# Unused matmuls ahead of the transposes of eight norms and of sixteen attention heads in a four-layer fp32 kernel

## The reference, cut to what matters

```python
xf = x.astype(jnp.float32)
y = xf * lax.rsqrt(jnp.mean(xf * xf, axis=-1, keepdims=True) + RMS_EPS)
return (y * g.astype(jnp.float32)).astype(x.dtype)
```

```python
p = jnp.where(mask, jnp.exp(s - m), 0.0)
return p / jnp.maximum(jnp.sum(p, axis=-1, keepdims=True), 1e-30)
...
o = g[..., 0:1] * o_c + g[..., 1:2] * o_s + g[..., 2:3] * o_w
```

## Time and profile before

| | |
|---|---|
| time, median of 3 runs | 2771.21 us (2769.89 to 2772.66) |
| the profiled execution's own time | 2782.96 us |
| its span, first to last instruction | 2781.2 us |
| PE busy | 2602.2 us (94%), 15074 records |
| PE weight loads busy | 2178.7 us (78%) |
| DVE, ACT, POOL busy | 1316.1, 398.8, 207.3 us |
| chain of work that ended last | PE 86%, DMA 7%, DVE 4%, ACT 2% |
| granted TensorE clock, mean | 0.939 |
| attention of section four, first scores to last combine | 2350.5 to 2493.3 us |

### The profile page before, as it was taken

How to read it: one execution, slowest core, us unless ns; L and a number is a source line. 1 busy time by engine, 2 the same in 40 slices (tenths; PEclk the granted TensorE clock), 3 DMA queues, 4 the chain that set the end, 5 groups by cost and what they waited for, 6 DMA issues and landing times.

```text
span 2781.2 us, 36057 instructions
## 1 busy us (share of the span) xinstructions
PE 2602.2 (94%) x15074; PEld 2178.7 (78%) x15074; DVE 1316.1 (47%) x2542; ACT 398.8 (14%) x1150; POOL 207.3 (7%) x208
## 2 busy tenths in 40 slices
PE   6998999999999899999999999983899999999998
PEld 5557999999998755899999998872466587875665
DVE  4734928878743473493887874316100001431001
ACT  2121111111100212111111111012000001320000
POOL 0000012222210000001222121000000000000000
PEclk9999999999999999999999999996899997559999
DMA  5222679999999332367999999840244422002432
GB/s 202 98 84 106 242 279 398 389 381 407 416 421 382 133 116 74 114 242 291 408 391 376 401 419 421 360 149 37 91 151 151 170 102 92 1 1 106 151 151 91
DMA packets 84755, 625.33 MB, mean 225 GB/s; under 512 B 10443, under 2 KB 12978, under 8 KB 14206
## 3 DMA queue, kind: packets, MB, share of 16 engines
q1 hardware_dynamic: 55580, 420.85, 39.3%
q0 software_dynamic: 28032, 201.54, 17.9%
q10 hardware_dynamic: 994, 0.82, 0.1%
HBM read 621.91 MB, written 1.06 MB: 224 GB/s over the span
## 4 chain that ended last, share of the span: by engine, by line
PE 86%; DMA 7%; DVE 4%; ACT 2%; issue 1%; SPq 0%; DVEq 0%; ACTq 0%; PEldq 0%
PE bank L716 19%; PE bank L741 16%; PE bank L466 9%; PE bank L480 8%; PE bank L488 8%; PE bank L454 8%; DMA weight_ring<-in_experts 5%; PE bank L730 5%; PE bank L418 3%; PE bank L838 2%; PE bank L904 2%; PE bank L906 1%; PE bank L536 1%; DMA arena<-in_expert_rows,choice_by_pair 1%; ACT arena L956 1%
## 5 line engine op out<-in xcount | busy, mean ns | idle before, releaser
L741 PE MATMUL bank<-arena,weight_ring 128*128 128x160 f32 x4096 | 576.2, 301 | 14.4 <-DMA weight_ring<-in_experts 14.3
L741 PEld LDWEIGHTS bank<-arena,weight_ring 128*128 128x128 f32 x4096 | 558.8, 190 | 25.3 <-DMA weight_ring<-in_experts 23.6
L716 PE MATMUL bank<-hidden_T,weight_ring 128*128 128x160 f32 x4096 | 570.6, 301 | 2.6 <-ACT arena L1065 2.3
L716 PEld LDWEIGHTS bank<-hidden_T,weight_ring 128*128 128x128 f32 x4096 | 561.3, 191 | 3.9 <-issue 3.8
L1615 DVE CUSTOM_DVE_ANT_0 arena<-arena 128x1024 f32<-128x1024 f32 x192 | 234.5, 1221 | 209.0 <-DMA arena<-in_expert_rows,choice_by_pair 208.8
L454 PE MATMUL bank<-weight_ring,hidden_T 128*128 128x512 f32 (+1 forms) x544 | 236.4, 592 | 36.4 <-DVE hidden_T L1734 34.3
L466 PE MATMUL bank<-hidden_T,weight_ring 128*128 128x256 f32 (+1 forms) x1088 | 249.6, 391 | 10.2 <-DMA weight_ring<-in_dense_h 6.1
L944 POOL DMA_INDIRECT arena<-in_expert_rows,choice_by_pair x192 | 200.2, 1043 | 789.0 <-DVE arena L1628 713.2
L466 PEld LDWEIGHTS bank<-hidden_T,weight_ring 128*128 128x128 f32 (+1 forms) x1088 | 208.5, 193 | 46.4 <-issue 7.0
L1628 DVE SCALAR_TENSOR_TENSOR arena<-arena,pair_weights 128x1024 f32<-128x1024 f32 x188 | 240.6, 1280 | 0.2
L480 PEld LDWEIGHTS bank<-hidden_T,weight_ring 128*128 128x128 f32 x1024 | 194.6, 190 | 52.9 <-issue 29.7
(11 more groups left out here) (313 smaller groups left out, 1832.4 us busy)
## 6 DMA issues: line engine op xcount, KB each, us to landing
weight_ring<-in_experts SPq DMA_DIRECT2D x256, 1024.0 KB, 9.2
weight_ring<-in_mlp SPq DMA_DIRECT2D x64, 1024.0 KB, 4.8
weight_ring<-in_dense_h SPq DMA_DIRECT2D x22, 2048.0 KB, 7.6
weight_ring<-in_dense_nsa SPq DMA_DIRECT2D x9, 2048.0 KB, 7.8
weight_ring<-in_dense_rg SPq DMA_DIRECT2D x7, 2048.0 KB, 7.6
arena<-in_expert_rows,choice_by_pair POOLq DMA_INDIRECT x192, 11.2
arena<-distance_bias_scratch SPq DMA_DIRECT2D x2, 768.0 KB, 5.6
residual<-in_x SPq DMA_DIRECT2D x1, 1024.0 KB
```

What stands on the lines that cost most here:

```text
L716: last = mm(bank[s % 2][:, 0:DT_TOK], w[:, k * P:(k + 1) * P], HT[:, k, 0:DT_TOK], start=k == 0, stop=k == KD - 1)
L741: last = mm(bank[4 + k // 2][:, (k % 2) * DT_TOK:(k % 2 + 1) * DT_TOK], w[:, k * P:(k + 1) * P], HACT[:, s, :], start=s == 0 and k % 2 == ...
```

## The change

Both additions are on PE alone and are read by nothing. In each of the eight norms, sixteen 128-column matmuls of the identity by itself go into bank 1 ahead of the wait for `norm_scaled`; the transposes overwrite that bank. In each of the sixteen heads, three matmuls of the identity by 256 columns of zeros go into bank 4, which the head's own transposes overwrite. To make this possible the two waits of `nsa_turn` change places: the one for `nsa_PT` comes first, then the three matmuls, then the one for `nsa_probs`. Line numbers of the kernel after are higher by 2 from L421 on, and by 4 behind `nsa_turn`, ACT and DVE included.

```diff
             def norm(count):
+                for _ in range(16):
+                    mm(bank[1][:, 0:P], ident[:], ident[:], start=True, stop=True)
                 for tt in range(TT):
 
                     pe.wait_ge(S["norm_scaled"], count * TT + tt + 1)
@@ -881,9 +883,11 @@
             def nsa_turn(h):
 
-                pe.wait_ge(S["nsa_probs"], h + 1)
                 if h:
                     pe.wait_ge(S["nsa_PT"], h)
+                for _ in range(3):
+                    mm(bank[4][:, 0:T], ident[:], zrow[:, 0:T], start=True, stop=True)
+                pe.wait_ge(S["nsa_probs"], h + 1)
```

## The result

| | before | with the change |
|---|---|---|
| time, median | 2771.93 us (2769.89 to 2781.58, 4 runs) | 2730.53 us (2728.52 to 2731.61, 4 runs) |
| ratio to before | | 0.9838, 95% interval 0.982 to 0.9857 |
| span of the profiled execution | 2781.2 us | 2729.8 us |
| mean granted clock | 0.939 | 0.973 |

The forecast was 2732 us, in a range from 2712 to 2757. The ratio is a gain of 45 us with an interval of 40 to 50; the medians differ by 41.

The account below looks back on a forecast made before the run. The prediction took TensorE at half its clock to bound the attention. Gains of 26 (attention), 9.5 and 3 (norms) and 1 (behind the attention) sum to 39.5 us: 2771.2 - 39.5 = 2732 us, range 2712 to 2757.

Parts of the forecast that it names:

- The bound: Attention of sixteen heads: TensorE at half its clock bounds the 143 us stage, busy for 138.6 of them.
- What raises the clock: TensorE: unbroken work on all rows raises it, zeros and transposes included; expected within the first one or two heads.
- The rule against it: Trainium skill: transposes don't engage the full clock, leaving a head's unbroken stretch 2.56 us, not 4.27; rival's chance 0.06.
- What lets it fall: TensorE: idle time or thin work, as in the compression, where 4.00 us at 1.00 came before 9.80 at 0.50.
- The price of a head: Attention, with the unused matmuls: a head costs 11.29 us at 1.2 GHz, 6.12 us at 2.4 GHz.
- The share at the low clock: Attention: 0.3 of the time at 1.2 GHz, bounds 0.05 and 0.6; stage gain 26 us.
- the formula: Attention time: sixteen heads at a rate weighting 11.29 and 6.12 us by clock share, plus 3.1 us; forecast 116.6.
- The norms behind a projection: Four norms after output projections: identities hidden in 4.5 us of idle time, clock holds; gain 9.5 us.
- The norms behind a barrier: Four norms behind a barrier: transposes 0.8, 0.8 and 2.0 us later in three, faster dense work; together +3 us.
- Behind the attention: Output projection after the attention, cold for 3.5 us: half of up to 1.8 + 0.7 us gained, +1.
- The sum: Whole kernel: 26 + 9.5 + 3 + 1 = 39.5 us gained, giving a median of 2732 us.

Follow-up runs that it names:

- first trace of before: The profile of the unchanged kernel that the prediction read: profiled execution 2782.96 us, span 2781.2 us.
- split runs: The change with each head's unused matmuls in two places: two and two of 256 columns, 0.9841 to before; three and three of 128 columns, 0.9828.
- heads only: The kernel before plus only the three unused matmuls per head and the exchanged waits, no identities in the norms: 0.9875 to before.
- second trace of before: The kernel before, unchanged, profiled once more: 2774.26 us, span 2772.5 us.

## Why the prediction was right

- **The bound.** TensorE at half its clock in the attention, nothing else near: right. With the clock up TensorE was still the bound, busy for 110.6 of 112.3 us, and neither ACT's copies nor the waits took over.
- **What raises the clock.** Work on all rows, zeros and transposes included: shown, by 64 rows that did not do it and by twelve transposes that did. The rule against it fell. How long the work must be unbroken was not tested apart.
- **What lets it fall.** The prediction read this off the compression's products, and that row bears less than was put on it. Its 4.0 us at 1.00 hold mostly the 48-column records of L454 ahead of the products. And the same 256 records took 13.57 us in the first trace of before, 10.54 in the second, and 10.30 in the kernel after, where the clock stood at 1.00 from 2319.3 to 2329.5 us (timeline of before, then of the kernel after):

```profile
2333.36 13.57 PE L853 MATMUL bank<-arena,weight_ring 64*64 64x45 f32 x256
```

```profile
2319.26 10.30 PE L855 MATMUL bank<-arena,weight_ring 64*64 64x45 f32 x256
```

So thin work does not always let the clock fall: 10 us of it passed at 1.00. That the thin stretch of a head does is shown by the split runs, not by that row. What makes it fall in one head and not in the next stays open, and so does which part of the stretch counts: its values use all rows, with 65 columns each.
- **The price of a head.** 6.12 us at the full clock was forecast, and 6.07 measured. That switches between row groups cost the same 0.2 us at either clock carried this; with them halved it would have been 5.6. The chain after shows it again: eight L908 records take 1.04 us, of which 0.85 are streaming, and at half the clock before they took 1.90, of which 1.71.
- **The share at the low clock.** I chose 0.3, and it was 0.28 in the trace. This was a choice between 0.05 and 0.6, and the least grounded number of the sum; that it came so close is luck. The stage gained 30.5 us, not 26, the largest miss. With 0.28 the formula gives 16 / (0.28/11.29 + 0.72/6.12) + 3.1 = 115.4, the trace 112.3. The formula spreads the low clock over all heads, but 8.7 us of it lie ahead of the first rise, over the first scores and the first head's transposes. Between the second head's transposes and the fifteenth's, six falls are 20 of 88.6 us, a share of 0.23; with that the formula gives 6.84 us a head, and 6.81 were measured.
- **The norms behind a projection.** 9.5 forecast, 9.4 (6 to 13) measured. From the transposes to the dense work 1.2 us were won each instead of 0.7, and the clock held in all four. The parts did not come out as forecast, and that the sum did is partly luck. Read from the first sum of squares to a point 60 records into the dense work, the four norms won 2.9, 3.1, 3.0 and 3.7 us against the first trace of before, 12.7 in all, and 2.4, 2.9, 3.1 and 1.2 against the second, 9.6. There the clock rose by itself ahead of section four's dense work, so half of the 5.0 us was not there to be won.
- **The norms behind a barrier.** +3 forecast, 2.5 measured with a wide interval. The delays were put at 0.8, 0.8 and 2.0 us. In the trace, barrier to transposes took 5.3 us (4.8 before), 4.7 (4.8 before) and 6.4 (3.7 before): 0.5, none and 2.7. What I had not seen is that the clock can still be up at the barrier, so that the identities cost only 3.8. Read to the same point, sections two to four give +2.7, +3.6 and -1.7 us against the first trace of before, and +2.5, +1.2 and -1.7 against the second: 4.6 or 2.0.
- **Behind the attention.** +1 forecast. In the trace of the kernel after, the projection began cold again; in heads only, and in the second trace of before, it began at 1.00. It is a matter of where the last fall lies, and no gain is shown.

The windows view of the output projection behind the attention in the kernel after answers to the earlier trace rows:

```profile
2449.70:2454.10 4.40, 4.39 (x5) 1.85 (x6) 0.00 (x0) 0.00 (x0) 0.00 (x0) 0.50 0.00 0
```

The sum was 39.5 us, and the gain 45 (40 to 50) by the ratio: 4 to 5 of the missing us are the stage's. By the medians the gain is 41, and the forecast lies 1.5 us from the median after. That is closer than its parts are, of which the stage alone was off by 4.5.

## What to carry to other kernels

A stage in which TensorE is "busy" all the time but stands at 0.50 in the clock row can be made faster by giving TensorE more to do, if the added work uses all rows. Here it stood next to full-row work that was there already, or, in the split kernels, partly by itself; which of the two is better was not tested. Price it by splitting a cycle into streaming, which halves, and switches between row groups, which don't; then ask of the thin stretch between two full-row blocks whether the clock will last through it, and cut that stretch in two rather than make the blocks longer. Fill only idle time that is longer than the filling takes at the clock it will find: behind dense work 3.7 us, behind a barrier up to 6.5.

## What the runs showed of the hardware that I had not expected

- Unused matmuls on 64 rows ran in part beside scores on the other 64 rows, and cost 1.35 us instead of 2.56 in every other head. They left the clock at 0.50 but for one short stretch.
- The same 256 records of the compression took 10.3 to 10.5 us in eight of the thirteen traces and 13.6 in five. All five are of kernels without identities in the norms, but two others without them took the short time. Whether the identities have a part in it is not shown.
- Two executions of the kernel before differ by 8.7 us in their traces with the same attention stage to 0.1 us; the difference is in how often and where the clock fell elsewhere.
- The clock could be held at 1.00 for 90 us of an attention whose own work, left alone, keeps it at 0.50, by eight records of unused work in a head.
